# Moving the matrix-memory chain of a two-block kernel in among the tiles of its output projection, and splitting that projection by rows

## What is computed

```python
z = rmsnorm_2(h, norm1_g) @ w_in
q, k, v, o, gates, u = jnp.split(z, [W, 2 * W, 3 * W, 4 * W, 4 * W + 2 * H], axis=-1)
qk = silu(causal_dwconv(concatenate([q, k]), conv_qk_w))
li, lf = gates[..., :H], log_sigmoid(gates[..., H:])
hm = mlstm_chunkwise(q, k, v, li, lf)                     # two chunks of 128 tokens
hm = hm * rsqrt(mean(hm * hm) + RMS_EPS) * mlstm_norm_g * sigmoid(o)
ys = s5_groups(u, ...)       # scan, then gelu, then ab = y @ glu_w; ab[:16] * sigmoid(ab[16:])
h = h + concatenate([hm, ys]) @ w_out
```

## Time and profile before

| | us |
|---|---|
| median of 3 runs | 4291.25 (4291.14 to 4295.61) |
| the profiled execution | 4292.4 |
| its span, first to last instruction | 4290.6 |
| PE busy | 4166.8 |
| DVE busy | 3144.6 |
| ACT busy | 2311.3 |
| POOL busy | 550.3 |

### The profile page before, as it was taken

The page is one execution under the profiler, slowest core; times in us unless marked ns, Lnnn a source line. Parts: engine busy times, 40 slices in busy tenths (PEclk is TensorE's granted clock), DMA queues, the critical chain, the costliest instruction groups (busy, mean ns, idle before and its releaser), DMA issues.

```text
span 4290.6 us, 88408 instructions
## 1 busy us (share of the span) xinstructions
PE 4166.8 (97%) x28580; PEld 3860.1 (90%) x28580; DVE 3144.6 (73%) x5354; ACT 2311.3 (54%) x4097; POOL 550.3 (13%) x541
## 2 busy tenths in 40 slices
PE   8999999999999999999999978999999999999998
PEld 8889999999999988778888868999999998888887
DVE  6467677885999755775769958778689995556655
ACT  4345545766656555555553353466755664555554
POOL 4111010000222211111100001000012221111110
PEclk9999999999999999999999989999999999999999
DMA  6434555666666666776655524656666666667664
GB/s 244 132 104 143 177 181 190 205 204 201 189 191 188 193 218 216 234 268 220 228 204 183 176 89 141 201 179 206 206 188 191 189 192 212 216 217 236 217 218 162
DMA packets 278941, 831.21 MB, mean 194 GB/s; under 512 B 31024, under 2 KB 98352, under 8 KB 275504
## 3 DMA queue, kind: packets, MB, share of 16 engines
q1 hardware_dynamic: 274320, 812.77, 59.0%
q10 hardware_dynamic: 4512, 17.06, 1.1%
HBM read 779.37 MB, written 50.33 MB: 193 GB/s over the span
## 4 chain that ended last, share of the span: by engine, by line
PE 89%; DVE 7%; ACT 2%; DMA 1%; issue 1%; SPq 0%; DVEq 0%; ACTq 0%; POOL 0%
PE psum L1426 18%; PE psum L1428 18%; PE psum L1427 18%; PE psum L414 10%; PE psum L415 10%; PE psum L416 10%; DVE sb_w_lo L1912 2%; PE psum L397 1%; PE psum L1518 1%; DVE sb_work L1203 1%; DVE sb_work L1197 0%; DVE sb_work L1196 0%; DMA sb_raw<-in_w_q 0%; DMA sb_raw<-in_w_proj 0%; ACT sb_w_hi L1647 0%
## 5 line engine op out<-in xcount | busy, mean ns | idle before, releaser
L1647 ACT CAST sb_w_hi<-sb_raw 128x512 fp32r<-128x512 f32 x2736 | 1691.7, 621 | 1774.0 <-PE psum L1428 1079.3
L1912 DVE TENSOR_TENSOR sb_w_lo<-sb_raw,sb_w_hi 128x512 fp32r<-128x512 f32 x2736 | 1865.5, 703 | 980.6 <-ACT sb_w_hi L1647 971.0
L1426 PE MATMUL psum<-sb_act_hl,sb_w_hi 128*128 128x256 f32 x6224 | 1776.3, 285 | 49.2 <-DVE sb_w_lo L1912 35.9
L1428 PE MATMUL psum<-sb_act_hl,sb_w_lo 128*128 128x256 f32 x6224 | 1767.2, 284 | 0.0
L1427 PE MATMUL psum<-sb_act_hl,sb_w_hi 128*128 128x256 f32 x6224 | 1766.6, 284 | 0.0
L1426 PEld LDWEIGHTS psum<-sb_act_hl,sb_w_hi 128*128 128x128 f32 x6224 | 1200.7, 193 | 63.0 <-issue 40.1
L1427 PEld LDWEIGHTS psum<-sb_act_hl,sb_w_hi 128*128 128x128 f32 x6224 | 1200.4, 193 | 0.8 <-issue 0.5
L1428 PEld LDWEIGHTS psum<-sb_act_hl,sb_w_lo 128*128 128x128 f32 x6224 | 1200.2, 193 | 0.0
L414 PE MATMUL psum<-sb_w_hi,sb_act_hl 128*128 128x512 f32 x2048 | 800.0, 391 | 13.8 <-DVE sb_w_lo L1912 13.7
L415 PE MATMUL psum<-sb_w_lo,sb_act_hl 128*128 128x512 f32 x2048 | 798.3, 390 | 0.0
L416 PE MATMUL psum<-sb_w_hi,sb_act_hl 128*128 128x512 f32 x2048 | 798.1, 390 | 0.0
(11 more groups left out here) (329 smaller groups left out, 2961.8 us busy)
## 6 DMA issues: line engine op xcount, KB each, us to landing
sb_raw<-in_u SPq DMA_DIRECT2D x512, 512.0 KB, 3.7
sb_raw<-in_v SPq DMA_DIRECT2D x512, 512.0 KB, 3.5
sb_raw<-in_w_z SPq DMA_DIRECT2D x82, 512.0 KB, 4.2
sb_raw<-in_w_gates SPq DMA_DIRECT2D x64, 512.0 KB, 3.5
sb_raw<-in_w_out SPq DMA_DIRECT2D x64, 512.0 KB, 3.5
acts_mid<-sb_acts_out SPq DMA_DIRECT2D x256, 128.0 KB, 4.4
sb_acts_in<-acts_mid SPq DMA_DIRECT2D x256, 128.0 KB, 3.3
sb_raw<-in_w_proj SPq DMA_DIRECT2D x56, 512.0 KB, 3.5
```

The costliest lines, as they stand in the source:

```text
L1426: pe.matmul(ps, w_h, src[:, k, 0:T], start=start and kk == 0, stop=False)
L1428: mm = pe.matmul(ps, w_l, src[:, k, 0:T], start=False, stop=stop and kk == 3)
L1647: act.copy(w_hi[:, c, :], raw[:, 2 * par + c // 2, (c % 2) * 512:(c % 2) * 512 + 512]).then_inc(hi_ready, 1)
L1912: dve.tensor_tensor(w_lo[:, c, :], raw[:, 2 * par + c // 2, (c % 2) * 512:(c % 2) * 512 + 512], w_hi[:, c, :].bitcast(F32), ALU.subtract). ...
```

## The change

1. `out2` becomes `out2a` and `out2b`, eight tiles each. `out2a` takes rows 1024 to 2047 of `w_out` (state-space), `out2b` rows 0 to 1023 (matrix memory). One tile holds two output tiles of 128 channels over eight k-blocks, so it has 48 matmuls too; each is added to two rows of `x1` at once (`first_half`, `second_half`). `out2a` reads `ys_hi`, `ys_lo`; `out2b` reads `act_hl`.
2. The matrix memory's work on values, gates, keys and the first four states moves into steps 11 to 40 of `z2`, the gated unit into steps 32 to 39; the rest of the chain runs as steps 1 to 7 of `out2a`, in batches over whole banks. Normalisation is a scale per token from squares that ACT accumulates. `dve_mix` and `act_mix` (gate, split) come behind `out2a`'s last tile.
3. The skip `d * u` becomes a diagonal matmul (`through`), `y_leave` goes, and ACT applies Gelu per group. The sum of squares becomes 16 matmuls.
4. q and k change places in `z2`'s tile order; SP loads `x1` in two halves; `act_weights` makes two gain tiles at each of eight steps.

```diff
-          ("z2", 41), ("out2", 16), ("wq2", 16), ("u2", 128), ("v2", 128)]
+          ("z2", 41), ("out2a", 8), ("out2b", 8), ("wq2", 16), ("u2", 128), ("v2", 128)]
...
         def pe_mlstm(pe):
+            for step in range(8):
+                if step == 1:
+                    scores2()
+                    pe.wait_ge(st_out, 4)
+                    states(pe, range(4, 8))
+                if step == 2:
+                    turn_weights()
+                if step == 3:
+                    pe.wait_ge(st_out, 8)
+                    local_sums(range(6), (2, 3, 6, 7, 4, 5))
+                if step == 4:
+                    pe.wait_ge(num_out, 2)
+                    local_sums((6, 7), (2, 3))
+                    pe.wait_ge(num_out, 6)
+                    state_sums()
+                if step == 7:
+                    pe.wait_ge(hm_ready, 1)
+                    for k in range(8):
...
+        def dve_mix(dve):
             dve.wait_ge(o_gate_ready, 1)
             for k in range(8):
+                dve.wait_ge(hmt_done, k // 2 + 1)
+                dve.scalar_tensor_tensor(mix[:, k, :], psum[:, 2 + k // 2, (k % 2) * T:(k % 2) * T + T], c_mlstm[:, k:k + 1], z_o[:, k, :],
+                                         ALU.mult, ALU.mult).then_inc(mix_ready, 1)
+            for k in range(8):
+                dve.wait_ge(mix_hi, k + 1)
+                ins = dve.tensor_tensor(act_hl[:, k, T:2 * T], mix[:, k, :], act_hl[:, k, 0:T].bitcast(F32), ALU.subtract)
+                if k % 2:
+                    ins.then_inc(act_ready, 1)
...
+        def dve_gates(dve, link, step):
+            if step == 11:
...
+            if step == 21:
+                dve.wait_ge(cum_done, 1)
...
+            if step == 25:
+                dve.wait_ge(row_done, 2)
...
+            if step == 26:
+                dve.tensor_reduce(d_max, decay, AX.X, ALU.max)
...
+            if step == 40:
+                dve.wait_ge(kt_done, 1)
...
         def pe_s5(pe):
...
+                pe.matmul(psum[:, 6 + j % 2, 0:T], through[:, j, :], z_u[:, j, :], start=False, stop=True, skip_group_check=True).then_inc(ys_done, 1)
...
-                if step == 3:
-                    total_of_block()
-                if step == 5:
+                if 2 <= step < 6:
+                    sum_of_block(step - 2)
+                if step == 4:
                     turn_root()
+                if step == 12:
+                    pe.wait_ge(xs_used, 3)
+                    turn_gates(pe)
+                if step == 20:
+                    pe.wait_ge(xs_used, 5)
+                    sum_gates(pe)
+                if step == 24:
+                    pe.wait_ge(xs_used, 6)
+                    gate_rows(pe)
+                if step == 32:
+                    pe.wait_ge(xs_used, 8)
+                    pe.wait_ge(glu_ready, 1)
+                    for j in range(4):
+                        gated_unit(j, 2 + j)
+                if step == 36:
+                    pe.wait_ge(glu_out, 4)
+                    turn_values(pe, range(0, 4), (2, 3))
+                    for j in range(4, 7):
+                        gated_unit(j, j)
+                if step == 37:
+                    gated_unit(7, 7)
+                if step == 38:
+                    pe.wait_ge(glu_out, 6)
+                    turn_values(pe, range(4, 8), (4, 5))
+                if step == 39:
+                    turn_keys(pe)
+                if step == 40:
+                    pe.wait_ge(kw_ready, 1)
+                    pe.wait_ge(vt_out, 8)
+                    pe.wait_ge(glu_out, 8)
+                    states(pe, range(4))
...
-            return steps + [(86, lambda: act_weights(act)), (100, lambda: act_s5_loads(act))]
+            return steps + [(84 + 2 * n, lambda n=n: act_weights(act, n)) for n in range(8)] + [(100, lambda: act_s5_loads(act))]
...
         def act_s5(act, root):
...
+                if step == 36:
+                    act.wait_ge(ys_in, 8)
+                    high(0)
+                if step == 37:
+                    gate(range(4, 7))
+                    values_out(act, range(0, 4), (2, 3))
+                if step == 38:
+                    gate((7,))
                 if step == 39:
+                    values_out(act, range(4, 8), (4, 5))
+                if step == 40:
+                    high(1)
...
+            def x_rest():
+                sp.wait_ge(ys_split, 2)
+                sp.dma_start(x1[:, 0:8], x_mid[:, 0:8]).then_inc(x_again, 16)
+            stream("z2", a["w_z2"], between={2: first_tables, **{4 * j: lambda j=j: table_back(j) for j in range(2, 8)}, 40: x_top})
+            stream("out2a", a["w_out2a"], between={2: x_rest})
+            stream("out2b", a["w_out2b"])
...
-            pe_glu(pe)
-            pe_mlstm(pe)
-            gemm("out2", acts=split_of(5))
+            gemm("out2a", halves=2, half_rows=True, steps_between=pe_mlstm(pe), acts=[(ys_split, 1), (ys_split, 2), (ys_split, 2), (ys_split, 2)], src=(ys_hi, ys_lo))
+            gemm("out2b", halves=2, half_rows=True, acts=[(act_ready, 18), (act_ready, 20), (act_ready, 20), (act_ready, 20)])
...
-            for pair in (6, 7):
-                smooth(act, pair)
-            act_glu(act)
-            act_mlstm(act)
-            stage("out2")
+            smooth(act, 7)
+            states_out(act, range(4))
+            act.wait_ge(tile_out, evac["out2a"])
+            act.activation(z_o, z_o, ACT.Sigmoid).then_inc(o_gate_ready, 1)
+            stage("out2a", steps_between=act_mlstm(act), begun=True, upcoming="out2b")
+            act_mix(act)
+            stage("out2b", begun=True)
...
+            def first_half(i, par):
+                m = (2 * i + 8) % 16
+                dve.wait_ge(x_again, 48 if i < 4 else 64)
+                dve.wait_ge(output_root_known, 1)
+                if i == 7:
+                    dve_mix(dve)
+                for k in (m, m + 1):
+                    dve.scalar_tensor_tensor(x1[:, k, :], x1[:, k, :], c_fin[:, k:k + 1], output_root, ALU.mult, ALU.mult).then_inc(x1_scaled, 1)
```

More of the change, by code:

```diff
@@ L987, in pe_s5 @@
                 yield
-        def pe_glu(pe):
-            pe.wait_ge(glu_ready, 1)
-            for j in range(8):
-                pe.wait_ge(y_gelu, 1)
-                if j >= 2:
-                    pe.wait_ge(glu_out, j - 1)
-                for part in range(2):
-                    mm = pe.matmul(psum[:, 6 + j % 2, part * T:part * T + T], glu_w[part][:, j, :], y_g[:, j, :], start=True, stop=True)
-                mm.then_inc(glu_done, 1)
         def act_s5_steps(act):
@@ L1064, in act_s5, with gate, high @@
         def act_s5(act, root):
+            def gate(some):
+                for j in some:
+                    act.wait_ge(glu_done, j + 1)
+                    act.activation(glu_gate[:, j, :], psum[:, 2 + j if j < 4 else j, T:2 * T], ACT.Sigmoid).then_inc(glu_sig, 1)
+            def high(half):
+                some = slice(4 * half, 4 * half + 4)
+                act.wait_ge(glu_out, 4 * half + 4)
+                act.copy(ys_hi[:, some], z_u[:, some]).then_inc(ys_hi_ready, 1)
             for step in range(1, 41):
@@ L1067, in act_s5 @@
                     act_s5_inputs(act)
+                if step in (3, 4):
+                    for j in range(4 * (step - 3), 4 * (step - 3) + 4):
+                        act.activation(through[:, j, :], ident, ACT.Copy, scale=c_d[:, j:j + 1]).then_inc(through_made, 1)
                 if step == 5:
-                    root(5)
-                if step == 6:
                     act.wait_ge(root_turned, 2)
@@ L1073, in act_s5 @@
                         act.copy(token_root[:, c:c + 1], psum[:, 2, c * P:c * P + 1]).then_inc(root_cols, 1)
+                for j in range(8):
+                    if step == 8 + 4 * j:
+                        act.wait_ge(ys_done, j + 1)
+                        act.activation(y_g[:, j, :], psum[:, 6 + j % 2, 0:T], ACT.Gelu).then_inc(y_gelu, 1)
+                if step == 8:
+                    root(5)
+                if step == 14:
+                    act.wait_ge(ml_in, 1)
+                    act.activation(soft, soft, ACT.Exp, scale=-1.0).then_inc(ml_out, 1)
+                if step == 16:
+                    act.wait_ge(ml_in, 2)
+                    act.activation(soft, soft, ACT.Ln).then_inc(ml_out, 1)
+                if step == 27:
+                    act.wait_ge(ml_in, 3)
+                    act.activation(e_out, e_in, ACT.Exp).then_inc(ml_out, 1)
+                if step in (28, 29):
+                    act.wait_ge(decay_in, 1)
+                    for u in range(4 * (step - 28), 4 * (step - 28) + 4):
+                        ins = act.activation(decay[:, u, :], decay[:, u, :], ACT.Exp, bias=neg_m[:, u:u + 1])
+                    if step == 29:
+                        ins.then_inc(decay_ready, 1)
+                if step == 33:
+                    gate(range(4))
                 if step >= 33:
@@ L1258, in dve_s5 @@
                         turn_back(j)
```

(24 more changed lines are left out.)

494 lines of the change are left out of this document (258 added, 236 removed).

## The result

Over four runs each the changed kernel takes 4246.48 us (4244.80 to 4248.10) and the kernel before 4291.19 (4289.41 to 4295.61): a ratio of 0.9894, 95% interval 0.9881 to 0.9906. The forecast was 4245.0, in a range of 4233 to 4264. The profiled execution took 4244.8 us with a span of 4243.2, 47.4 less than the span before.

A forecast was written before the change was run, and what follows sets the result against it. PE was taken as the bound, idle or slow in the hole between z2 and out2, with DVE pacing much of z2. Terms summed to -48.5 from 4292.4; 1.15 lower for the median, 2 for hops: 4245 us, range 4233 to 4264.

The forecast's parts named there:

- v1: Stage v1: ACT's gain copies in pairs fit between casts and remove PE's wait of 1.99 us; -2.0.
- Head of z2: Start of z2: DVE loses a 7.37 us reduction, gets two products of 2.35, PE gets 16 matmuls; -2.0 net.
- Middle of z2: z2 before PE's last state-space outputs: DVE sets the pace, gains gate work and loses y_leave; +4.7, PE's additions stay under DVE.
- 1.0 of clock: z2's middle: PE's clock falls after waits in steps 25 and 26; 1.0 us taken as visible, bounds 0 and 3.
- waits of "some 2.5 us" in steps 25 and 26: z2's middle: PE was expected to wait some 2.5 us in each of these two steps.
- Tail: z2 from PE's last state-space outputs: PE-bound, 8.1 of added PE work less shrunken waits and 0.4 back; +7.4.
- rival that ACT binds there by its table switches: Steps 37 to 39 of z2: six table switches cost double, about 8 us back, total -40; chance 0.05.
- The first rival: Steps 36 to 40 and 1 to 5: PE waits 2 us at each of eight exchanges, 16 back, total -32; chance 0.15.
- out2: From z2's end to out2's end: 174.3 us becomes 116.7 with the chain among out2a's tiles and out2b at 5.75 a tile; -57.6.
- wait of 6.2: Ahead of out2b: PE waits 6.2 us because dve_mix stands behind the w_lo set of out2b's tile 0; 1.6 of clock lost after.
- 2 us set aside for hops: Added to the forecast time for semaphore hops in some forty new exchanges, 0.05 us each.
- low end of 4233: Lower bound of the forecast range: no clock loss in z2 and half the out2b wait.

The follow-up runs named there:

- experiment 1: The kernel before with only the 16 gain tiles of stage v1 made in pairs at eight steps: 4287.44 us, ratio 0.9991 (0.9981 to 1.0001).
- experiments 2 to 10: Nine variants of the changed kernel, 4238.79 to 4257.0 us; a stretch of z2's middle with unchanged instructions took 61.08 to 61.11 us in their traces, 59.61 in the changed kernel's.
- experiment 7: The changed kernel with eight more 128x128 products on DVE (1.66 us) beside the decay matrix in z2's middle: 4248.77 us; 1.59 of 1.66 show.
- experiment 8: The changed kernel with gate-row matmuls doubled in z2's middle and key transposes doubled in its tail, both on PE: 4250.52 us; 0.83 and 0.51 show.
- experiments 9 and 10: The changed kernel with the last Gelu and q/k Silus as Sigmoid, 4248.08 us; and with an added Exp and Gelu in steps 37 to 39, 4250.96 us.
- experiment 3: The changed kernel with GpSimd's squares and sums in the second block cut from 256 to 8 columns: 4248.39 us in one run; out2b evacuations 5.76 apart.
- experiment 2: The changed kernel with the mix put ahead of the low parts of out2b's first weights in DVE's queue, ACT's splits reordered too: 4242.77 us, ratio 0.9886.
- experiment 5: The changed kernel with out2b's high products of x_hl moved from DVE to ACT, DVE's low products a tile later: 4243.53 us, ratio 0.9884.

## Why the prediction came out as it did

*v1.* Forecast -2.0; -2.0 between the two profiled executions, -1.4 in experiment 1, where the wait of 1.99 is gone but whose interval doesn't exclude nothing.

*Head of z2.* -2.0 against -2.1, by the table. It wasn't tried alone, so that the lost reduction is the cause is argued from the trace.

*Middle of z2.* 4.7 and 1.0 of clock against 5.4, but not in these shares: in the profiled execution the granted clock is 1.00 from `outputs(0)` to the wait of 3.65, and from that wait to `outputs(7)` it is 7.4 us against 7.5 before. So all of the 5.4 is work and waits, 0.7 more than forecast, and the clock cost nothing more than before. In the traces of experiments 2 to 10 it cost 1.5 in front of the 3.65. That DVE sets the pace and every microsecond on it is paid, experiment 7 shows for one place; that PE's additions stay free there is half true (experiment 8). Of the waits of "some 2.5 us" in steps 25 and 26 the first is 0.70 (before tile 25) and the second 2.43 (before tile 26). The 3.65 before tile 34 is none of them: the kernel before waits 2.38 and 2.21 before tiles 33 and 34, where DVE's turning back and convolutions stand.

*Tail.* 7.4 against 7.8. The rival that ACT binds there by its table switches falls with experiments 9 and 10: all six loads gone give 0.35 us. The Trainium skill, "ScalarE: Activation LUTs", section "What ACT_TABLE_LOAD costs", has a switch at about 2.66 us, of which 1.38 are a drain. The trace doesn't agree: from 2487.67 to 2490.71 two loads and two functions fit in 3.04 us, and the function starts 1.29 behind its load.

*The relay.* The first rival, that waits of some 2 us survive at each exchange, has no row: the largest waits in out2a are 1.14 and 0.85, and in steps 36 to 40 of `z2` PE has none above 0.15.

*out2.* Here the failed step is: "today's products on `x_hl` take 0.8 in the hardware loop and down to 0.48 written out, as out2b's are; 2.2 to 2.9 us a tile with 2.4 of `w_lo` stay under 5.75". I had two prices in a row and gave the difference to the form of the instruction. It belongs to the neighbour, and the neighbour reaches further than these products. Two lines of the kernel before, DVE's and GpSimd's timeline in `out2`, which the prediction didn't lay beside each other:

```profile
2630.92 0.79 DVE L2122 SCALAR_TENSOR_TENSOR sb_x_hl<-sb_work,sb_cols,sb_x_hl  x1 [0.15 <-DVE sb_x_hl L2120]
```

```profile
2630.70 0.74 POOL L1841 TENSOR_TENSOR sb_work<-sb_work 128x256 f32<-128x256 f32 x1
```

In both kernels GpSimd begins its squares as soon as DVE has evacuated, and so runs just beside DVE's products. Written out, a low product took 0.89 in out2b (1.78 for two), and 0.44 when GpSimd was light (experiment 3). By their starts DVE's tile is 2.96 of `w_lo`, 0.71 for the evacuation, 0.89 for the high and 1.71 for the low products: 6.27, above PE's 5.75. The forecast's upper end was 5.3 (2.9 and 2.4). It holds with 0.8 for each low product, so a better price for these alone would not have found the miss. What it put at nothing is that GpSimd slows the rest as well: 0.56 on `w_lo`, which it had at 2.4, and 0.36 on the high products (0.53 when GpSimd was light). The Trainium skill, "SBUF — State Buffer", section "SBUF: two separate sides", has VectorE and GpSimd share one pair of ports, so that a VectorE instruction with two SBUF inputs waits while a GpSimd one that reads SBUF holds it. The trace agrees for the low products, with 0.89 against 0.44, and for the first `w_lo`; the high products have one large input in SBUF and are slower too (0.97 against 0.61 for two), which this sentence doesn't cover.

Before, the slowdown was hidden: a tile of `out2` had one such pair of products on DVE and came every 5.75 us (the windows). out2b's tiles run over half the k-blocks for two of the old output tiles, so the same PE time has two pairs. That is the term that was mis-sized. The new course is 3.5 us longer than forecast (120.15 against 116.7); 3.0 of it are the six slow tiles, the rest mostly the clock in front of them. By the same edges the old course was 175.0 and not 174.3, which takes 0.7 off, and the row misses by 2.7.

The wait of 6.2 was right in place, size and cause: 5.96, and moving the order of DVE's and ACT's work took it to 2.3. Its clock came nearly as forecast, 1.6 said: out2b's first two tiles took 13.5 us, where two at 5.75 are 11.5, so 2.0 were lost; in experiment 2, at full clock and with the wait of 0.29, they took 12.1.

That the total is as close as it is (4245.0 for 4246.5) owes something to chance. The steps of the table give 45.8, where the forecast's gave 48.5. In the profiled execution 1.9 us from a stage that the change doesn't touch hid most of that; the median is 1.7 us above that execution, and the 2 us set aside for hops, which no run here measures, met it. And the range's low end of 4233 isn't reached by what it names: no clock loss and half the wait take 1.0 and 3.1 off 4245.

## What to carry to other kernels

Where one instruction has two prices in a trace, look at what the other engines do at that moment before giving the difference to its form; a VectorE evacuation that releases GpSimd's work puts that work beside its own next instruction. When a relay is filled with tiles, the gain ends where a filling stage becomes bound by an engine that was hidden, so count each engine's time per tile again with the new tile's share of evacuation. Moving work away from the bound engine may give back less than its price, if the neighbour then runs beside something else (experiment 5). And of the wait that stays, ask first what stands ahead of the late work in its own queue: here its order alone was worth 4 us, and the clock of the stage behind it 1.4 more.
